# Three projection steps of an inverse's level together behind the masked product

## The chip, the cores and the metric

The kernel runs on one core of one Trainium2 chip. The metric is the device time of one execution in microseconds (us); three executions of the kernel before gave 1539.69 to 1544.26 us, median 1543.43. Engines: PE is TensorE (the matrix engine, with PEld its weight loads), DVE is VectorE, ACT is ScalarE, POOL is GpSimd, SP issues the DMAs.

## The reference, cut to what matters

The reference is one inference step of a decoder layer for a prompt of 512 tokens and 8 decode samples. The part that the change touches is the input projection and the RWKV-7 recurrence:

```
proj = h @ w_in                       # columns r | k | v | loras | pool | gates
xs   = cur + (prev_rows - cur) * mu_shift       # token shift
# per head, per token:
sa = S @ kk;  S = S*w - sa (kk*a)^T + v k^T;  y = S @ r
```

The prompt's recurrence is computed in chunks of 64 tokens. In a chunk the dependence of each token on the earlier ones is a unit triangular 64 x 64 matrix, which must be inverted, for 16 heads and 8 chunks.

## The kernel before, in words

The recurrence stage runs over c = 0..7, two heads (128 partitions) at a time; one turn of the loop is a **slot**, written out once for each engine in that engine's own order (functions `slot(c)` for PE, ACT, DVE and POOL). Engines wait for each other by counting semaphores only, and each engine takes its instructions in the order in which they are written. So what stands behind a waiting PE instruction waits too.

A slot on PE does two things at once. It computes the recurrence of head pair c in many small matrix products, whose results ACT, DVE and POOL have to take up before the next can run; and between these it projects the columns of the next pair, c + 1, which depend on nothing but the loaded weights. The projection is cut into **steps**: `kstep` is one of 8 slices of the contraction, six matmuls (fp32 split in a high and a low part), and there are three projections of 8 steps, 24 in all: steps 0 to 7 make K, 8 to 15 make R, 16 to 23 make V. `dense(n)` issues the next n steps. All three go to the same accumulation buffer, `PJ[0]`. So `project` waits at the first step of each (0, 8, 16) for two counts: `w_lo` (the weights are split) and `xs`, which DVE raises when it has finished reading the projection before out of `PJ[0]`. For step 8 that is the evacuation of K: two ACT operations (`shift`, lines 727 and 729) and one DVE operation (`XK`, line 870), in this order, and ACT starts once step 7 is done.

The **inverse** is built in levels lv = 0..5. Level lv from 1 on has:

- the masked product (`mm_x`, line 619), which needs `TI`, the transposed inverse, copied out by ACT at the level before (line 801), and the masked matrix `MO`, made by POOL;
- `dense(2)`; meanwhile DVE adds the identity to the product and writes `XI` (line 952; the trace names it RAW, whose memory it uses);
- at level 2 alone 16 small products (`mm_nv`);
- the wait for `XI`; the transpose's product (`mm_ti`, line 641, levels 1 to 4), from which ACT copies `TI`; and the inverse's product (`mm_tt`, line 645), from which DVE copies `TT` (line 962);
- an extra: at level 1 `center` (line 564) and at level 2 `variance` (line 568) of the pair before, from slot 1 on; at level 4 `ss` (line 520) of the next pair;
- `dense(1)`, at level 5 `dense(2)`.

After level 5 PE waits for `TT`, runs `mm_w` (line 659), one step (16, with the wait for R's evacuation), and after some products the chain of the eight states, with one step behind each of seven of them. At the slot's end ACT copies `WK` out (line 831), and PE's next slot waits for that. Slot 7 has no next pair: its `dense` does nothing. The projections ahead of slot 0 run one after the other with nothing between.

Of the kernel before, what the change touches and what calls it, by code (L numbers as in the profile page):

```python
# [46 lines left out]
LEVELS = 6  # L47
# [51 lines left out]
def build(nc, i, o):  # L99
    es = ExitStack()  # L100
    with es:
        sems = {}

        def S(name):
            if name not in sems:
                sems[name] = es.enter_context(nc.semaphore(name))
            return sems[name]
# [302 lines left out]
        with ExitStack() as sc:  # L410
# [47 lines left out]
            def num(c, q):  # L458
                return B_RKV + 3 * c + q
# [57 lines left out]
            def _(pe):  # L517
# [5 lines left out]
                def project(n, pj, k0, k1):  # L523
                    if k0 == 0:
                        pe.wait_ge(S("w_lo"), n + 1)
                        after(pe, "xs", n if n > 1 else 0)
                    for k in range(k0, k1):
                        mm = kstep(pe, PJ[pj], n % 3, k, Hh, Hl, k, k == 0, k == KT - 1, nb)
                    if k1 == KT:
                        mm.then_inc(S("prj"), 1)  # L530
# [9 lines left out]
                def za(c):  # L540
                    pe.wait_ge(S("sigw"), c + 1)
                    small(PJ[1], WL[64:P, :], TWA[64:P, :]).then_inc(S("mm_za"), 1)

                def ss(c):
                    pe.wait_ge(S("kks"), c + 1)
                    pe.wait_ge(S("alpha"), c + 1)
                    after(pe, "lnv", c - 1)
                    small(PJ[1], bones, SM[:]).then_inc(S("mm_ss"), 1)
# [12 lines left out]
                def center(c, nxt):  # L561
                    pe.wait_ge(S("yf"), c + 1)
                    pe.wait_ge(S("alpha"), c + 3) if nxt else pe.wait_ge(S("gte"), KT)
                    pe.matmul(PJ[1][:, 0, :], ctr, YF[:], start=True, stop=True).then_inc(S("mm_gn"), 1)

                def variance(c):
                    pe.wait_ge(S("yq"), c + 1)
                    pe.matmul(PJ[1][:, 1, :], bones, YQ, start=True, stop=True).then_inc(S("mm_gn"), 1)

                def slot(c):  # L570
# [3 lines left out]
                    def dense(n):  # L574
                        if not nxt:
                            return
                        for st in range(done[0], done[0] + n):
                            project(num(c + 1, st // KT), 0, st % KT, st % KT + 1)
                        done[0] += n
# [27 lines left out]
                    for lv in range(LEVELS):  # L607
                        if lv == 0:
                            pe.wait_ge(S("mo0"), c + 1)
                            pe.wait_ge(S("tr_ev"), 4 * c + 1)  # L610
                        else:
                            pe.wait_ge(S("mo"), (LEVELS - 1) * c + lv)
                            if lv == 1:
                                pe.wait_ge(S("xi"), LEVELS * c + 1)
                            else:
                                pe.wait_ge(S("ti"), (LEVELS - 2) * c + lv - 1)
                        for j in range(NJ):
                            for h in range(2):
                                mm = pe.matmul(B[0][HH[h], j * C:(j + 1) * C], MO[HH[h], lv % 2, j, :],  # L619
                                               I2[HH[h], :] if lv == 0 else TI[HH[h], j, :], start=True, stop=True)  # L620
                        mm.then_inc(S("mm_x"), 1)
                        if lv == 0:
                            if nxt:
                                za(c + 1)
                            continue
                        dense(2)
                        if lv == 2:
                            pe.wait_ge(S("tr_ev"), 4 * c + 4)
                            for j in range(NJ):
                                for h in range(2):  # L630
                                    mm = pe.matmul(B[3][HH[h], j * C:(j + 1) * C], KP[HH[1 - h], j, 0, :], VT[HH[1 - h], j, :],
                                                   start=True, stop=True)
                            mm.then_inc(S("mm_nv"), 1)
                        pe.wait_ge(S("xi"), LEVELS * c + lv + 1)
                        if lv == 1:
                            pe.wait_ge(S("tr_ev"), 4 * c + 3)
                        pe.wait_ge(S("tt"), LEVELS * c + lv)
                        if lv < LEVELS - 1:
                            for j in range(NJ):
                                for h in range(2):  # L640
                                    mm = pe.matmul(B[1][HH[h], j * C:(j + 1) * C], TT[HH[h], j, :], XI[HH[h], j, :], start=True, stop=True)
                            mm.then_inc(S("mm_ti"), 1)
                        for j in range(NJ):
                            for h in range(2):
                                mm = pe.matmul(B[2][HH[h], j * C:(j + 1) * C], XI[HH[h], j, :], TT[HH[h], j, :], start=True, stop=True)  # L645
                        mm.then_inc(S("mm_tt"), 1)
                        if lv == 1 and prv:
                            center(c - 1, nxt)
                        if lv == 2 and prv:
                            variance(c - 1)  # L650
                        if lv == 4 and nxt:
                            ss(c + 1)
                        dense(2 if lv == LEVELS - 1 else 1)

                    pe.wait_ge(S("tt"), LEVELS * (c + 1))
                    pe.wait_ge(S("nv_ev"), c + 1)
# [60 lines left out]
                for c in range(KT):  # L717
                    slot(c)
# [1083 lines left out]
```

## Time and profile before

| | |
|---|---|
| median of 3 executions | 1543.43 us |
| the profiled execution's own time | 1543.15 us |
| its span (first to last instruction) | 1541.4 us |
| PE busy | 1268.9 us, 82% of the span |
| DVE busy | 715.8 us, 46% |
| ACT busy | 471.1 us, 31% |
| POOL busy | 86.8 us, 6% |
| mean granted clock of TensorE | 0.920 |

The recurrence stage's eight slots last from about 198 to 676 us. Busy shares are means over stages with different limits; what one edit is worth is read in its own stage, from the order of starts on PE.

### The profile page before, as it was taken

How to read it: one execution, taken by the hardware profiler on the slowest of the kernel's cores; microseconds unless marked ns; L12 is line 12 of the kernel's file. 1: busy time of each engine (PE TensorE's matmuls, PEld its weight loads, DVE VectorE, ACT ScalarE, POOL GpSimd, SP SyncE). 2: the span in 40 equal slices, each digit the busy share in tenths (PEclk: the TensorE clock that was granted, in tenths of full speed). 3: DMA queues.
4: the chain of work that ended last, by engine and by line, in shares of the span. 5: the costliest groups of instructions: out<-in, count | busy, mean ns of one | idle time of the engine just before them, and what ended most of it. 6: DMA issues, size and time to landing. Idle time of an engine off the chain costs nothing. (4 is left out here: it accounts for less than half of the span.)

```text
span 1541.4 us, 33797 instructions
## 1 busy us (share of the span) xinstructions
PE 1268.9 (82%) x14732; PEld 1120.8 (73%) x14732; DVE 715.8 (46%) x1106; ACT 471.1 (31%) x715; POOL 86.8 (6%) x145
## 2 busy tenths in 40 slices
PE   4896799999999999857079999913999999789953
PEld 1225788888888888747079999913999989789952
DVE  2102455555555555435943333176566666632216
ACT  0003543333433334233032222303444444422211
POOL 0000021020220211201000000000000000000000
PEclk9996999999999999978589999955999999989985
DMA  8762011011010110012143232221232223133221
GB/s 271 261 230 73 14 47 48 2 48 47 3 47 4 46 34 3 3 51 76 55 125 93 84 93 79 82 115 49 76 91 81 88 82 94 38 89 100 75 83 61
DMA packets 160379, 117.17 MB, mean 76 GB/s; under 512 B 6240, under 2 KB 144278, under 8 KB 159975
## 3 DMA queue, kind: packets, MB, share of 16 engines
q1 hardware_dynamic: 160273, 115.57, 24.4%
q8 instruction: 89, 1.46, 0.4%
q14 instruction: 17, 0.14, 0.0%
HBM read 108.40 MB, written 7.34 MB: 75 GB/s over the span
## 5 line engine op out<-in xcount | busy, mean ns | idle before, releaser
L194 PE MATMUL PJ<-Hh,Wh 128*128 128x260 f32 (+1 forms) x1088 | 244.1, 306 | 53.3 <-DVE Wl L1683 18.9
L194 PEld LDWEIGHTS PJ<-Hh,Wh 128*128 128x128 f32 x1088 | 173.1, 194 | 72.8 <-issue 31.2
L194 PE MATMUL PJ<-Hl,Wh 128*128 128x260 f32 (+1 forms) x1088 | 224.2, 288 | 0.0
L194 PE MATMUL PJ<-Hh,Wl 128*128 128x260 f32 (+1 forms) x1088 | 223.1, 287 | 0.0
L194 PEld LDWEIGHTS PJ<-Hl,Wh 128*128 128x128 f32 x1088 | 173.0, 193 | 0.0
L194 PEld LDWEIGHTS PJ<-Hh,Wl 128*128 128x128 f32 x1088 | 172.7, 193 | 0.0
L1683 DVE TENSOR_TENSOR Wl<-RAW,Wh 128x1024 fp32r<-128x1024 f32 (+1 forms) x68 | 80.9, 1194 | 100.9 <-ACT Wh L1623 96.2
L1623 ACT ACTIVATE Wh<-RAW 128x1024 fp32r<-128x1024 f32 (+1 forms) x68 | 70.1, 1036 | 111.4 <-PE PJ L194 103.7
L1703 DVE SCALAR_TENSOR_TENSOR ACC<-ACC,CP 128x512 f32<-128x512 f32 x88 | 66.1, 751 | 69.6 <-ACT ACC L1634 68.0
L1377 DVE TENSOR_TENSOR Wl<-RAW,Wh 128x1024 fp32r<-128x1024 f32 (+1 forms) x40 | 44.7, 1119 | 112.8 <-ACT Wh L1339 112.0
L194 PE MATMUL PJ<-SFh,Wh 128*128 128x260 f32 x352 | 71.9, 286 | 14.5 <-DVE Wl L1683 14.5
L194 PE MATMUL BB<-Hh,Wh 128*128 128x260 f32 x352 | 71.6, 284 | 0.0
L194 PE MATMUL PJ<-SFl,Wh 128*128 128x260 f32 x352 | 71.4, 285 | 0.0
L194 PE MATMUL PJ<-SFh,Wl 128*128 128x260 f32 x352 | 71.4, 285 | 0.0
L194 PE MATMUL BB<-Hl,Wh 128*128 128x260 f32 x352 | 70.9, 283 | 0.0
L194 PE MATMUL BB<-Hh,Wl 128*128 128x260 f32 x352 | 70.7, 283 | 0.0
L194 PEld LDWEIGHTS PJ<-SFh,Wh 128*128 128x128 f32 x352 | 55.0, 191 | 14.7 <-issue 14.7
L1476 PE MATMUL PJ<-CST,ACC 128*128 128x128 f32 (+1 forms) x80 | 15.5, 364 | 60.4 <-DVE XA L1548 57.6
L1057 POOL TENSOR_TENSOR MO<-BP,CST 128x512 f32<-128x512 f32 x40 | 54.5, 1362 | 104.1 <-PE BB L619 101.9
L962 DVE COPY TT<-BB 128x512 f32<-128x512 f32 x40 | 27.6, 691 | 66.2 <-PE BB L645 66.2
L1476 PEld LDWEIGHTS PJ<-CST,ACC 128*128 128x128 f32 (+1 forms) x80 | 11.5, 170 | 63.9 <-DVE XA L1548 59.7
L194 PEld LDWEIGHTS PJ<-SFl,Wh 128*128 128x128 f32 x352 | 55.1, 190 | 0.0
(305 smaller groups left out, 2421.0 us busy)
## 6 DMA issues: line engine op xcount, KB each, us to landing
RAW<-in_w_in_dram SPq DMA_DIRECT2D x46, 512.0 KB, 4.1
RAW<-in_ffn_up_dram SPq DMA_DIRECT2D x44, 512.0 KB, 3.8
RAW<-in_ada_w_dram SPq DMA_DIRECT2D x6, 2048.0 KB, 8.4
ACC<-in_ada_w_dram SPq DMA_DIRECT2D x6, 2048.0 KB, 8.0
RAW<-in_ffn_down_dram SPq DMA_DIRECT2D x16, 512.0 KB, 4.1
RAW<-in_w_branch_rwkv_dram SPq DMA_DIRECT2D x8, 512.0 KB, 4.1
RAW<-in_w_out_dram SPq DMA_DIRECT2D x8, 512.0 KB, 4.0
RAW<-in_ffn_down_dram SPq DMA_DIRECT2D x8, 384.0 KB, 3.4
```

Of the source, the lines that this page charges most:

```text
L194: mm = pe.matmul(out[:, b, 0:nb[b]], w[:, slot, kw, :], x[:, kx, c0:c0 + nb[b]], start=first and w is Wh and x is xh, stop=last and w is Wl)
L962: dve.tensor_copy(TT[:], bank8(2)).then_inc(S("tt"), 1)
L1057: pool.tensor_tensor(MO[:, lv % 2], BP[:, :, 0, :], rows8(CST[:, C_OFF + C * lv:C_OFF + C * (lv + 1)]), ALU.mult).then_inc(S("mo"), 1)
L1377: dve.tensor_tensor(Wl[:, slot, 0:kn], RAW[:, slot, 0:kn], Wh[:, slot, 0:kn].bitcast(F32), ALU.subtract).then_inc(S("w_lo"), 1)
L1476: mm = pe.transpose(PJ[t % 2][0:n, b, r * P:(r + 1) * P], delta[:, k, t * P:t * P + n], ident)
L1623: act.activation(Wh[:, slot, 0:kn], RAW[:, slot, 0:kn], ACT.Copy).then_inc(S("w_hi"), 1)
L1683: dve.tensor_tensor(Wl[:, slot, 0:kn], RAW[:, slot, 0:kn], Wh[:, slot, 0:kn].bitcast(F32), ALU.subtract).then_inc(S("w_lo"), 1)
L1703: dve.scalar_tensor_tensor(cv[:, 0:T], u[:, k:k + T], w, cv[:, 0:T], ALU.mult, ALU.add)
```

## The change

Two numbers. In levels 1 to 5 the first `dense` issues three steps instead of two, and the one behind the inverse's product issues none instead of one (levels 1 to 4), or one instead of two (level 5). The 24 steps of a slot, their order and the rest of the slot stay. The count by the end of each level is as before: 3, 6, 9, 12, 16.

```diff
                         if lv == 0:
                             ...
                             continue
-                        dense(2)
+                        dense(3)
                         if lv == 2:
                             ...
                         if lv == 4 and nxt:
                             ss(c + 1)
-                        dense(2 if lv == LEVELS - 1 else 1)
+                        dense(1 if lv == LEVELS - 1 else 0)
```

## Rows read from the trace of the kernel before

**Rows 1.** Windows, one slot: us, busy (count) per engine, PEclk, DMA share, GB/s.

```profile
320.00:382.00 62.00, 59.80 (x1132) 52.84 (x1135) 33.66 (x51) 22.43 (x36) 9.17 (x13) 1.00 0.11 31
```

**Rows 2.** Waits of PE from 200 to 630: us in total, times, longest.

```profile
PE BB L590 <- ACT WK L831: 9.1, 6, 1.5
...
PE BB L619 <- ACT TI L801: 1.9, 7, 0.3
```

**Rows 3.** Timeline of PE, slot 2, level 3: start, us, engine, line, operation.

```profile
342.39 1.15 PE L619 MATMUL BB<-TI,MO 64*64 64x64 f32 x32
343.47 0.51 PE L194 MATMUL PJ<-Hh,Wh 128*128 128x260 f32 x2
...
345.12 1.15 PE L641 MATMUL BB<-RAW,TT 64*64 64x64 f32 x32
...
347.16 0.48 PE L194 MATMUL PJ<-Hh,Wh 128*128 128x260 f32 x2
...
348.41 1.15 PE L619 MATMUL BB<-TI,MO 64*64 64x64 f32 x32 [0.27 <-ACT TI L801]
```

**Rows 4.** Timeline of ACT and DVE there: the evacuation of K.

```profile
345.23 0.70 ACT L727 ACTIVATE A<-PJ,PV 128x520 f32<-128x520 f32 x1 [4.35 <-PE PJ L194]
...
346.26 0.76 DVE L870 SCALAR_TENSOR_TENSOR XK<-PJ,OM,A 128x520 f32<-128x520 f32 x1 [1.98 <-ACT A L729]
```

**Rows 5.** Timeline ahead of slot 0: an evacuation between two projections.

```profile
161.41 0.76 DVE L870 SCALAR_TENSOR_TENSOR AL<-PJ,OM,A 128x520 f32<-128x520 f32 x1 [3.22 <-ACT A L729]
162.32 0.48 PE L194 MATMUL PJ<-Hh,Wh 128*128 128x260 f32 x2 [1.98 <-DVE AL L870]
```

**Rows 6.** Timeline of slot 0, levels 1 and 2, which have no extra.

```profile
210.22 1.10 PE L645 MATMUL BB<-TT,RAW 64*64 64x64 f32 x32
211.25 0.51 PE L194 MATMUL PJ<-Hh,Wh 128*128 128x260 f32 x2
...
212.17 1.15 PE L619 MATMUL BB<-TI,MO 64*64 64x64 f32 x32
```

**Rows 7.** Timeline of slot 7, level 3, where `dense` does nothing.

```profile
650.62 1.15 PE L641 MATMUL BB<-RAW,TT 64*64 64x64 f32 x32 [0.79 <-DVE RAW L952]
...
651.82 0.60 ACT L801 ACTIVATE TI<-BB 128x512 f32<-128x512 f32 x1 [3.92 <-PE BB L641]
...
652.56 1.15 PE L619 MATMUL BB<-TI,MO 64*64 64x64 f32 x32
```

**Rows 8.** Timeline, `center` in slot 7 without steps, then in slot 2 with one.

```profile
642.62 1.13 PE L564 MATMUL PJ<-YF,CTR 128*128 128x512 f32 x2
643.67 0.97 PE L619 MATMUL BB<-TI,MO 64*64 64x64 f32 x26
...
333.32 1.13 PE L564 MATMUL PJ<-YF,CTR 128*128 128x512 f32 x2
...
335.10 1.15 PE L619 MATMUL BB<-TI,MO 64*64 64x64 f32 x32
```

**Rows 9.** Timeline of slot 2, level 4: `ss`, and level 5's masked product.

```profile
353.17 1.14 PE L520 MATMUL PJ<-SM,CST 128*128 128x260 f32 x4
...
354.98 1.15 PE L619 MATMUL BB<-TI,MO 64*64 64x64 f32 x32
```

**Rows 10.** Timeline, level 5's end in slot 2, then in slot 7 without steps.

```profile
357.71 1.15 PE L645 MATMUL BB<-TT,RAW 64*64 64x64 f32 x32
...
360.45 1.96 PE L659 MATMUL BB<-AW,TT 64*64 64x128 f32 x32
...
658.36 1.15 PE L645 MATMUL BB<-TT,RAW 64*64 64x64 f32 x32 [0.78 <-DVE RAW L952]
...
660.30 0.87 PE L659 MATMUL BB<-AW,TT 64*64 64x128 f32 x12 [0.79 <-DVE TT L962]
```

**Rows 11.** Timeline of ACT at slot 2's end: the evacuation of V.

```profile
380.05 0.70 ACT L727 ACTIVATE A<-PJ,PV 128x520 f32<-128x520 f32 x1 [4.61 <-PE PJ L194]
```

**Rows 12.** Windows, the start of slot 5; columns as in rows 1.

```profile
506.00:509.00 3.00, 3.00 (x61) 2.67 (x53) 1.74 (x4) 0.00 (x0) 1.14 (x6) 0.52 0.73 202
```

## The prediction

> **What bounds the kernel now.** I read the windows by slot first, then who PE waits for, then the order of starts on PE in one slot, and last the evacuations on ACT and DVE beside it. In slot 2 PE is busy 59.8 us of 62 [rows 1], and in this stretch PE waits longest for the slot's end; inside the levels it waits only for `TI`, 0.27 us a slot [rows 2]. The reader is to see two things there. PE sets the pace, so time added to or taken from PE's own order is added to or taken from the kernel. And no wait for `XI` stands in the list of PE's waits for slots 0 to 6: two steps already cover it. A third step in that place has no wait to remove.
>
> The stall-free picture has one tight place, level 3. Step 7, the last of K, ends there at 345.12, and step 8, the first of R, starts at 347.16 [rows 3]. Between the two PE runs the transpose's and the inverse's product. In the same time ACT (345.23) and then DVE (346.26, 0.76 long) read K out of `PJ[0]`, until 347.02 [rows 4]. Step 8 may not start before this read is over. In the kernel before, the two products hide the evacuation, with 0.14 us to spare.
>
> **The change, part by part.** No instruction is added or removed; five steps a slot are moved, on PE alone, in slots 0 to 6. No DMA and no SP or POOL instruction is moved.
>
> Durations of the blocks. One step between small products costs 0.92 us (211.25 to 212.17 [rows 6]); two cost 1.65 (343.47 to 345.12 [rows 3]); so a further step in an existing block costs about 0.73.
>
> *Level 3.* Step 8 now stands right behind step 7 and must wait for the evacuation. The row that shows such a wait by itself is the one ahead of slot 0, where a projection follows another with nothing between: PE sat idle 1.98 us, and went on at 162.32, 0.15 after DVE's end at 162.17 [rows 5]. In slot 2, counted from the start of level 3's masked product (342.39), K is out at 4.63, so step 8 starts at 4.78 and ends 0.90 later at 5.68. I take 0.90 and not 0.92 since a step after a wait has a first group of 0.48 and not 0.51 [rows 3, 5]. Then come the transpose's and the inverse's product, and the next masked product directly. Slot 7 shows this sequence without any step: 650.62 to 652.56, 1.94 [rows 7]. The masked product of level 4 so starts at 5.68 + 1.94 = 7.62, where it started at 6.02 before (348.41 - 342.39 [rows 3]). That is 1.60 us later. The 0.27 that it waited for `TI` before is gone inside these numbers: in slot 7 the copy of `TI` starts 1.20 after the transpose's product and takes 0.60, which just fits into the 1.94 [rows 7].
>
> Bounds of this term: if the weights of the waiting step were loaded already, 0.15 less; if `TI` came as late as before, 0.27 more. 1.45 to 1.87, and I take 1.60.
>
> *Levels 1, 2 and 4, slots 1 to 6.* Here the moved step stood behind an extra. `center` with a step behind it took 333.32 to 335.10, 1.78 [rows 8]; `center` without one 1.05 in slot 7 [rows 8]. The difference, 0.73, is just what the step costs in its new place. No gain, no loss. `variance` at level 2 repeats the pattern. For `ss` with its step the trace has 1.81 (353.17 to 354.98 [rows 9]) and none without a step; 1.81 less one step of 0.92 to 0.73 gives 0.89 to 1.08 for it alone. The level changes by -0.19 to 0, and I take 0, by the nearest row, `center`.
>
> *Levels 1 and 2, slot 0.* Without an extra, the inverse's product plus a step took 212.17 - 210.22 = 1.95 [rows 6]. Without the step it takes 0.93: the 1.94 of rows 7 for both products, less 1.01 for the transpose's (2.04 for both in rows 3, less 1.03 for the inverse's in rows 6). That saves 1.02 and the third step costs 0.73: -0.29 each, -0.58 together.
>
> *Level 5.* Behind the inverse's product one step is left of two. `mm_w` needs `TT`, and slot 7 shows how late that is: 1.94 after the inverse's product, 0.79 of it idle [rows 10]. Product and one step take 2.74 - 0.73 = 2.01 [rows 10], so the copy is still covered, by 0.07. Were it not, 0.1 a slot. The three steps in front cost the 0.73 that is taken away behind. Step 15, which ends R, stays the instruction in front of `mm_w`, so R's evacuation and step 16's wait for it keep their distance.
>
> *What else might come late.* Level 4's `XI`: DVE has `TT` of level 3, two products for the key and `XI` in a row, four operations no longer than the 0.76 of rows 4. From the end of the inverse's product, at about 7.75 in the count above, they end by 10.8; PE asks for `XI` after the masked product and three steps, at 7.62 + 1.08 + 2.38 = 11.1. Covered. ACT's roots end earlier than R's evacuation starts by about a microsecond. After level 5 every wait is counted from PE's own work: ACT sat idle 4.61 us for PE before it read V out [rows 11], so the wait for `WK` moves along unchanged.
>
> **The sum.** Slots 1 to 6: 6 x 1.60 = 9.60. Slot 0: 1.60 - 0.58 = 1.02. Together 10.6 us, all on PE's order, against the profiled execution's own 1543.15: 1553.8. The median of the runs shown lies 0.3 above this execution, so I say 1554. Later stages start from the last slot and shift as a whole.
>
> **A rule against it: the clock.** The granted clock was 1.00 throughout slot 2 [rows 1], and it stayed at full speed after the 1.98 idle of rows 5: the next steps ran at their usual pace. But after the idle at slot 5's start it fell to 0.52 for some 3 us [rows 12]. By the Trainium skill, page "TensorE: Matmul & The Clock Gate", section "Why this matters for your kernels", idle gaps between bursts of matmuls send the array back to half rate. The trace bears this out at one of the slots' ends, with 1.5 us idle before it; the windows of the six other slots from 0 to 6 repeat the 1.00 of rows 1. The new gap of 1.9 is a second such place in each slot.
>
> **The rivals.**
>
> *Clock (0.08).* The clock falls at each of the seven new gaps. Price: half of 3 us at 0.52, 1.4 each [rows 12], 10 in all, on top of 10.6: 1564. For it: rows 12. Against it: rows 5, the very same gap with steps on both sides, and the six slots at 1.00.
>
> *The extras hide the seam (0.05).* The rise is smaller because behind `center`, `variance` and `ss` the seam of a block falls away as it does in slot 0: 18 places (three levels, six slots) of 0.29, less 5.2 us: 1549. For it: rows 6. Against it: rows 8 measure the place itself.
>
> *The slot's end absorbs it (0.05), the other side.* PE waits 1.5 for `WK` at each slot's end [rows 2]. If ACT's end of the slot were set by ACT's or DVE's own queue and not by PE, PE could be 1.5 late for nothing: 10.6 less 7 x 1.5 gives 1543, no change. It decides at one point: whether the copy of `WK` stays put when PE is late. Against it: the 4.61 idle of ACT for PE [rows 11].
>
> *The wait is not there (0.02), faster.* If the count that step 8 asks for were met already, level 3 would be one block of three: 1.08 + 2.38 + 1.94 = 5.40 against 6.02, -0.62 in seven slots, and -0.58 in slot 0: -4.9, 1538.3. Against it: rows 5, where DVE's read is what PE was released by.
>
> **How the numbers follow.** The forecast, 1554, has 0.80. Its own range is 1.45 to 1.87 a slot (9.6 to 12.6 us), the seam of `ss` (up to -1.3), level 5 (up to +0.7), and one clock fall more or less in an execution (1.4 each way; the runs of before span 4.6): 1550 to 1559. It leaves the clock rival out above and the others below, some 0.2 together. What a measurement can tell from no change is 0.3%, 4.6 us. Slower holds the forecast, the clock and the seams: 0.92. Same holds the absorption and half of what is odd: 0.05. Faster: 0.03.
>
> **What would show it.** In each of slots 0 to 6 a new wait of PE for DVE's `XK` at level 3, seven in number, 1.8 to 1.9 us each, 13 in sum. The wait for `TI` (1.9 in 7) gone. From level 3's masked product to level 4's 7.6 and not 6.0. Slots of 63.5 and not 61.9. Slot ends with the same 1.5 for `WK`. The forecast is wrong if `XK`'s evacuation ends earlier relative to step 7, if the wait for `WK` shrinks, if a seam behind an extra gives time back, or if the windows at level 3 show a clock under 1.

## The result

The changed kernel takes 1559.5 us in the median of four executions (1554.76, 1558.15, 1560.92, 1564.52) against 1543.8 before: a ratio of 1.011, interval 1.007 to 1.015. In a second comparison the changed kernel's median over five more executions is 1559.54 again, against 1542.26 for 17 of the kernel before; a third one, without the changed kernel, has 22 of the kernel before at 1541.68. So the change costs 15.7 us in the first comparison and 17.3 in the second, where 10.6 were forecast. The direction, the place and the wait are as forecast; the size is not, and the range (to 1559) missed it by half a microsecond.

The profiled execution of the changed kernel (its own time 1554.76, span 1553.0) agrees with the forecast to a microsecond, 11.6 over that of before. That is luck, as the times by stage below show: one must look into the stage that was changed, and not at the two spans.

Who PE waits for in the changed kernel, from 195 to 650, answers to [rows 2]:

```profile
PE PJ L194 <- DVE XK L870: 13.8, 7, 2.0
PE BB L590 <- ACT WK L831: 10.6, 7, 1.5
PE BB L666 <- DVE W L973: 2.3, 7, 0.3
```

The first line is new, in each of the seven slots with a next pair, 1.97 us each (forecast 1.8 to 1.9). `WK`'s wait is the same 1.52 a slot (the 9.1 of [rows 2] were for six, this is for seven). The wait for `TI` is gone.

PE in slot 2, level 3, answers to [rows 3]:

```profile
345.49 1.15 PE L619 MATMUL BB<-TI,MO 64*64 64x64 f32 x32
346.57 0.52 PE L194 MATMUL PJ<-Hh,Wh 128*128 128x260 f32 x2
...
350.27 0.48 PE L194 MATMUL PJ<-Hh,Wh 128*128 128x260 f32 x2 [1.97 <-DVE XK L870]
...
351.17 1.15 PE L641 MATMUL BB<-RAW,TT 64*64 64x64 f32 x32
352.15 1.10 PE L645 MATMUL BB<-TT,RAW 64*64 64x64 f32 x32
...
353.11 1.15 PE L619 MATMUL BB<-TI,MO 64*64 64x64 f32 x32
```

Step 8 starts 4.78 after the level's masked product, the two products follow it at 5.68, and level 4's masked product starts at 7.62: to the hundredth the working of the prediction. DVE's part of the evacuation, answering to [rows 4], ends at 350.13, 0.14 before step 8:

```profile
349.37 0.76 DVE L870 SCALAR_TENSOR_TENSOR XK<-PJ,OM,A 128x520 f32<-128x520 f32 x1 [1.99 <-ACT A L729]
```

`center` with no step behind it takes 337.12 to 338.18, 1.06 (forecast 1.05 [rows 8]). Level 5's copy of `TT` stays hidden, as worked out from [rows 10]: 2.00 from the inverse's product to `mm_w`, with no wait.

```profile
337.12 1.12 PE L564 MATMUL PJ<-YF,CTR 128*128 128x512 f32 x2
338.18 1.15 PE L619 MATMUL BB<-TI,MO 64*64 64x64 f32 x32
...
363.11 1.15 PE L645 MATMUL BB<-TT,RAW 64*64 64x64 f32 x32
365.11 1.96 PE L659 MATMUL BB<-AW,TT 64*64 64x128 f32 x32
```

Now the same place in slot 0:

```profile
218.53 0.48 PE L194 MATMUL PJ<-Hh,Wh 128*128 128x260 f32 x2 [1.97 <-DVE XK L870]
218.84 0.41 PE L194 MATMUL PJ<-Hl,Wh 128*128 128x260 f32 x2
219.09 0.58 PE L194 MATMUL PJ<-Hh,Wl 128*128 128x260 f32 x2
219.60 1.98 PE L641 MATMUL BB<-RAW,TT 64*64 64x64 f32 x32
221.37 1.64 PE L645 MATMUL BB<-TT,RAW 64*64 64x64 f32 x32
222.85 1.10 PE L619 MATMUL BB<-TI,MO 64*64 64x64 f32 x32
```

The wait is as long, but half a microsecond after step 8 has begun, the operations get longer: the transpose's product takes 1.77 and not 0.98 to the next. The windows (us, busy and count by engine, granted clock, DMA) show why, slot 0 first, then slot 2:

```profile
218.00:221.00 3.00, 2.47 (x32) 2.27 (x34) 0.38 (x1) 0.73 (x1) 0.00 (x0) 0.69 0.00 0
...
351.00:354.00 3.00, 3.00 (x96) 2.86 (x97) 0.70 (x2) 1.54 (x2) 0.00 (x0) 1.00 0.02 5
```

The granted clock averages 0.69 in slot 0's window: for a part of it TensorE ran at the lower of its two levels, 1.2 GHz and not 2.4. In slot 2 it did not. Such a change to the lower level is called a fall here. Counting the falls by the starts of the masked products (level 3's to level 4's is 7.6 without and 9.1 with one; a slot's last to the next slot's first is 33.4 without and 35.0 with one, 32.4 and 33.8 for slot 6) gives the whole account. "Slots" is from slot 0's first masked product to slot 7's, in the profiled execution; each profile is of one execution, the median of all:

| kernel | falls at level 3 | falls at slot ends | slots, us | median, us |
|---|---|---|---|---|
| before | 0 | 1 (slot 4) | 432.5 | 1541.7 |
| before, second profile | 0 | 1 (slot 6) | 432.0 | |
| changed | 3 (0, 5, 6) | 3 (0, 1, 2) | 450.6 | 1559.5 |
| changed, second profile | 3 (0, 5, 6) | 3 (0, 1, 2) | 450.6 | 1559.5 |
| step 8 put back | 0 | 2 (0, 3) | 433.6 | 1540.3 |
| level 3 alone | 2 (0, 3) | 3 (0, 3, 4) | 450.8 | 1559.2 |
| gap filled | 0 | 3 (4, 5, 6) | 446.0 | 1556.9 |
| gap longer | 7 | 4 (0, 2, 4, 6) | 462.8 | 1571.5 |
| before, ends filled | 0 | 0 | 430.8 | 1538.3 |
| changed, both filled | 0 | 0 | 441.6 | 1549.4 |
| new order on ACT | 0 | 0 | 423.9 | 1532.9 |

The medians come from three comparisons, in which the kernel before had 1543.8, 1542.3 (changed again, step 8 put back, level 3 alone, gap filled) and 1541.7 (the last four of the table), so a difference across them is good to a microsecond or two, and the slots' times are the sharper measure.

The stage itself lost 450.6 - 432.5 = 18.1 us: 10.6 by the new wait, as forecast, and 7.5 by five more falls of 1.5. In the first pair of profiles 4.1 of it were hidden by a slow start of the kernel before (its slot 0 began at 204.20, in its second profile at 200.39; the changed kernel's at 200.07 and 202.09) and 2.4 by stages after the slots, which the change does not touch.

### The profile page after: what moved, and what is told of

Read it like the earlier page. It is cut to its first block and busy times, and to the rows that moved or that the text cites. A ratio compares the mean times of both kernels' runs of the same rounds, so it can differ in the third digit from the quotient of the medians.

```text
span 1553.0 us, 33797 instructions
## 1 busy us (share of the span) xinstructions
PE 1271.1 (82%) x14732; PEld 1122.2 (72%) x14732; DVE 715.8 (46%) x1106; ACT 472.0 (30%) x715; POOL 85.6 (6%) x145
## 3 DMA queue, kind: packets, MB, share of 16 engines
q8 instruction: 89, 1.46, 0.4%
## 5 line engine op out<-in xcount | busy, mean ns | idle before, releaser
L194 PE MATMUL PJ<-Hh,Wh 128*128 128x260 f32 (+1 forms) x1088 | 237.7, 300 | 66.7 <-DVE Wl L1683 18.8
```

The costliest lines, as they stand in the source:

```text
L194: mm = pe.matmul(out[:, b, 0:nb[b]], w[:, slot, kw, :], x[:, kx, c0:c0 + nb[b]], start=first and w is Wh and x is xh, stop=last and w is Wl)
```

## The experiments

**Put step 8 back.** Levels 1, 2, 4 and 5 changed, level 3 as before.

```diff
-                        dense(3)
+                        dense(2 if lv == 3 else 3)
...
-                        dense(1 if lv == LEVELS - 1 else 0)
+                        dense(1 if lv in (3, LEVELS - 1) else 0)
```

> The changed kernel with one step put back: at level 3 two steps in front and one behind the inverse's product, as before; levels 1, 2, 4 and 5 stay changed. Theory 1 (all of the loss is the wait of step 8 for K's evacuation, and the clock falls that this gap brings): the time of the kernel before less 0.6 us, 1543, with the spread of the kernel before (about 5 us), and no wait of PE for XK. Theory 2 (part of the loss lies in the three joined steps of the other levels): 2 to 6 us above the kernel before, 1546 to 1550.

Measured 1540.3 against 1542.3 (ratio 0.998, 0.997 to 0.999), twelve executions from 1536.1 to 1541.8. In PE's waits `XK` does not appear, and `TI` is back:

```profile
PE BB L590 <- ACT WK L831: 10.6, 7, 1.5
PE BB L666 <- DVE W L973: 2.4, 7, 0.3
PE BB L619 <- ACT TI L801: 1.9, 7, 0.3
```

So all of the loss is at level 3. The joined steps of the other levels cost nothing. The two levels of slot 0 did give their share: 5.49 and 6.16 us, against 5.67 and 6.42 in the second profile of the kernel before. The gain of 2.0 us is more than the 0.6 worked out, and the interval (1.1 to 4.9 us) does not reach down to 0.6. Falls do not explain the rest, since this profile has two and those of the kernel before have one each; what does is open.

**Level 3 alone.**

```diff
-                        dense(2)
+                        dense(3 if lv == 3 else 2)
...
-                        dense(2 if lv == LEVELS - 1 else 1)
+                        dense(2 if lv == LEVELS - 1 else 0 if lv == 3 else 1)
```

> The kernel before with level 3 alone changed (three steps in front, none behind). Theory 1: 7 x 1.60 = 11.2 us from the wait, plus clock falls at the new gap of 1.5 us each in some of the seven places, so 1555 to 1565, spread about 10 us, as the changed kernel. Theory 2: 2 to 6 us less than the changed kernel.

Measured 1559.2 (1555.75 to 1563.8), ratio 1.011, 1.009 to 1.014: the changed kernel's loss. One step moved in one level of seven slots costs what the whole change costs. Its profile has one fall fewer and yet the same 450.8 us in the slots: level 4 takes 6.70 us and not 6.55, since with two steps in front the inverse's product waits a little for `XI`, and slot 0's levels 1 and 2 do not give their 0.6.

**The changed kernel again.**

> The changed kernel once more, to see how its executions spread and to have a second profile. Theory 1: median 1556 to 1562; from level 3's masked product to level 4's either 7.6 or 9.1 us in each slot, the 9.1 in other slots than in the first profile (0, 5 and 6 there), with a granted clock under 1 there. Rival (falls belong to certain slots, say to their DMAs): the 9.1 again in slots 0, 5 and 6.

Measured 1559.54 (1558.38 to 1560.62). The half of the expectation on where the falls are was wrong: they are in the very same places as in the first profile, 0, 5 and 6 at level 3 and the ends of 0, 1 and 2. They are not spread at random. But neither are they bound to these slots: with level 3 alone changed they come in 0 and 3. This profile also has the place of [rows 5], the gap of 1.97 ahead of slot 0, and here the clock does fall behind it (0.50 in the window):

```profile
158.41 0.49 PE L194 MATMUL PJ<-Hh,Wh 128*128 128x260 f32 x2 [1.97 <-DVE AL L870]
```

```profile
160.00:163.00 3.00, 3.00 (x16) 3.00 (x15) 2.46 (x3) 1.46 (x2) 0.00 (x0) 0.50 0.00 0
```

So it does, 1.4 to 1.5 us behind that gap, in five of the eleven profiles. The row on which the forecast took the falls as zero does not show the rule, but one of two outcomes that both occur.

**Fill the gap.** Ahead of step 8 (`KT` is 8) PE does useless work in the time that it would wait: 14 matmuls into the other accumulation buffer, which nobody reads. The three waits in front are for that buffer and the weights.

```diff
                         for st in range(done[0], done[0] + n):
+                            if st == KT:
+                                pe.wait_ge(S("w_lo"), num(c + 1, R_) + 1)
+                                pe.wait_ge(S("alpha"), c + 2)
+                                after(pe, "lnv", c)
+                                for _ in range(14):
+                                    pe.matmul(PJ[1][:, 1, 0:260], Wh[:, num(c + 1, R_) % 3, 0, :], Hh[:, 0, 0:260], start=True, stop=True)
```

> The changed kernel, with 14 matmuls of 128x260 whose result nobody reads in the new gap, between step 7 and the wait of step 8. They take 14 x 0.122 = 1.7 us, less than the 1.97 of the gap, so step 8 starts when it did. Theory 1: the 10.6 us of the wait stay, the clock falls at the gap go: median 1554 to 1556, spread near the kernel before's, and level 3's masked product to level 4's is 7.6 in all seven slots. Rival (the excess over 10.6 us is not the clock, or falls are not brought by the idle gap): median 1559 and a spread of 10 us, as the changed kernel.

Slot 0 in this kernel, the filler at 219.00:

```profile
216.37 1.15 PE L625 MATMUL BB<-TI,MO 64*64 64x64 f32 x32
...
219.00 1.83 PE L583 MATMUL PJ<-Hh,Wh 128*128 128x260 f32 x14
221.14 0.48 PE L194 MATMUL PJ<-Hh,Wh 128*128 128x260 f32 x2 [0.31 <-DVE XK L876]
...
222.05 1.15 PE L647 MATMUL BB<-RAW,TT 64*64 64x64 f32 x32
...
223.98 1.15 PE L625 MATMUL BB<-TI,MO 64*64 64x64 f32 x32
```

Step 8 starts 4.77 after the masked product, as without the filler, and the next masked product at 7.61, in all seven slots. The falls at level 3 are gone, and the slots are 4.6 us shorter than in the changed kernel, three falls' worth. Three falls remain at the slots' ends, which this kernel does not fill, as many as the changed kernel has there. The median, 1556.9 (1550.9 to 1558.1), fell by 2.7 alone and lies a microsecond above the expected 1554 to 1556; with five and six executions this is not resolved further.

**A longer gap.**

```diff
                         for st in range(done[0], done[0] + n):
+                            if st == KT:
+                                pe.wait_ge(S("kks"), c + 2)
```

> The changed kernel with a longer gap: step 8 also waits for ACT's square of the key, which ends 0.76 us after the read of K (347.78 against 347.02 in the kernel before's slot 2). Theory 1 (each gap costs its length, and brings a clock fall of 1.5 us the more often the longer it is): 7 x 0.76 = 5.3 us over the changed kernel's 1559.5 by the wait alone, and more than the three of seven gaps with a fall, up to seven: 1565 to 1571; level 3's masked product to level 4's is 8.4 without and 9.9 with a fall. Rival (a fall goes with certain places in time, not with the length of the gap): 5.3 us and no more falls, 1564 to 1565.

Measured 1571.5 (1565.4 to 1575.2), 12.0 over the changed kernel and half a microsecond above the expected range. In the slots it is 12.2: the waits grew from 13.8 to 18.5, 4.7 and not the 5.3 expected, and there are five more falls of 1.5. PE's waits first, then windows in slot 1 before, in and after the gap:

```profile
PE PJ L194 <- ACT SM L760: 18.5, 7, 2.6
```

```profile
281.00:284.00 3.00, 2.85 (x45) 2.53 (x44) 1.38 (x2) 0.11 (x1) 1.29 (x1) 1.00 0.00 0
284.00:287.00 3.00, 0.50 (x4) 0.51 (x5) 0.76 (x1) 1.58 (x3) 0.00 (x0) 1.00 0.00 0
287.00:290.00 3.00, 3.00 (x57) 2.85 (x57) 0.00 (x0) 0.74 (x2) 0.00 (x0) 0.62 0.02 5
```

The clock is 1.00 in the gap and falls after it. All seven gaps of 2.64 us bring a fall, where 1.97 brought three of seven. The rival, that length does not matter, is out; that the place in time matters too is shown further on.

**Fill the slots' ends, in the kernel before and, with the filler of level 3, in the changed one.**

```diff
                     mm.then_inc(S("t_wk"), 1)
+                    if nxt:
+                        pe.wait_ge(S("gte"), c + 2)
+                        for _ in range(10):
+                            pe.matmul(PJ[1][:, 1, 0:260], Wh[:, num(c + 1, R_) % 3, 0, :], Hh[:, 0, 0:260], start=True, stop=True)
```

> The kernel before with 10 matmuls of 128x260, read by nobody, behind each slot's last product, in the 1.52 us in which PE waits for WK. They take 1.2 us. The kernel before's profile has one clock fall there in seven. Theory 1: none here, every slot 61.9, time 1 to 2 us under the kernel before's, 1540 to 1541.5. Rival (filling changes nothing): 1542.3.

> The changed kernel with both gaps filled, the one of level 3 and the one at the slot's end. Theory 1: no clock fall among the slots 0 to 6, each of 1 to 5 takes 63.5 us, and the time over that of the kernel before with its slot ends filled is the bare wait, 7 x 1.60 less 0.6, 10.6 us, so 1551 to 1553. Rival (something else than wait and clock falls): the difference stays at 14 us or more.

The kernel before with its ends filled: 1538.3 (ratio 0.998, 0.996 to 1.000). The changed kernel with both filled: 1549.4, and its waits of PE are

```profile
PE BB L672 <- DVE W L983: 2.4, 7, 0.3
PE PJ L194 <- DVE XK L880: 2.2, 7, 0.3
...
PE BB L596 <- ACT WK L841: 0.4, 2, 0.2
```

Neither has a fall between slot 0 and slot 7. Their difference is 11.1 in the medians and 441.6 - 430.8 = 10.8 in the slots: the bare wait, forecast as 10.6. What the changed kernel loses to falls is then 450.6 - 441.6 = 9.0 in the slots, six falls of 1.5 (10.1 in the medians), and the kernel before 1.7 and 1.2 in its two profiles (3.4 in the medians). Both filled kernels came out 1.6 to 1.7 below their expected ranges (1540 to 1541.5 and 1551 to 1553), while the slots took what was expected.

**The kernel before, a second profile.**

> The kernel before once more, for a second profile of its clock falls at the slots' ends (one of seven in the first). With its ends filled it was 3.4 us faster in the median, which at 1.6 us a fall is two of them: so one to three falls of seven here, none inside the levels (level 3's masked product to level 4's 6.02 in all), and 432 to 436 us from slot 0's first masked product to slot 7's. If there is none, the 3.4 us of the filling came from somewhere else.

One fall, at slot 6's end, 432.0 in the slots. So falls explain 1.2 to 1.7 of the 3.4 that the filling gave; the rest is inside that ratio's interval (0.5 to 5.9 us) and its cause is open.

**A version that beats both.** Step 8 as before the change, and on ACT:

```diff
-                        shift(num(c + 1, V_), 0, mu(c + 1, V_))
                     act.wait_ge(S("mm_y"), c + 1)
                     ...
                     act.activation(WK[:], B[2][:, 0:C], ACT.Copy).then_inc(S("wk"), 1)
+                    if nxt:
+                        shift(num(c + 1, V_), 0, mu(c + 1, V_))
```

> A version that should beat both: step 8 behind the inverse's product as in the run with one step put back (1540.3), and on ACT at the slot's end YF and WK copied ahead of the evacuation of V, not behind it. PE's next slot then starts 1.0 us earlier (380.75 instead of 381.79 in slot 2), as long as the evacuation of V, 0.5 us later, does not hold up DVE's first masks of the next slot, which have about 1 us of slack. Theory: 7 x 1.0 = 7 us less, and fewer clock falls at the shorter gap: 1531 to 1534. If the masks are late instead: 1537 to 1541.

Measured 1532.9 (1531.6 to 1537.7), ratio 0.995, 0.994 to 0.997. ACT at slot 1's end, answering to [rows 11]: `WK` is now copied ahead of V's evacuation, not behind it.

```profile
310.76 0.60 ACT L827 ACTIVATE YF<-BB 128x512 f32<-128x512 f32 x1 [3.69 <-PE BB L696]
311.94 0.22 ACT L830 ACTIVATE WK<-BB 128x64 f32<-128x64 f32 x1 [0.58 <-PE BB L704]
312.06 0.69 ACT L727 ACTIVATE A<-PJ,PV 128x520 f32<-128x520 f32 x1
```

PE's wait is

```profile
PE BB L590 <- ACT WK L830: 2.9, 7, 0.4
```

2.9 us in seven in place of 10.6, a slot takes 60.88 and not the 61.93 of the kernel with step 8 put back, and there is no fall at a gap this short, 0.42 us.

## Why the prediction was wrong

*What bounds the kernel* held: PE sets the pace, and all that is added to its order appears in the time.

*Level 3* held to the hundredth (4.78, 5.68, 7.62), with its release row from [rows 5] and its sequence without steps from [rows 7]. Only the "0.14 us to spare" is misread: PE goes on 0.14 after DVE's end in the changed kernel too, where it waits, and 0.15 after in [rows 5]. So this is the time from the release to the first matmul, and the kernel before had nothing to spare: its two products fit the evacuation exactly. *Levels 1, 2 and 4* held: 1.06 for `center`, 6.54 for level 4 to 5 against 6.57. *Slot 0* gave 0.27 and 0.24 for the 0.29 each (second profile of before, 5.67 and 6.42, against 5.40 and 6.18). *Level 5* held. *The wait for `WK`* moved along unchanged, so the absorption rival is out, and so are the hidden seams and the missing wait. The clock rival came true by near half: three falls at the seven new gaps, each at about the price it named. The sum, 10.6, is what the two filled kernels differ by, 10.8 to 11.1.

What failed is the step "a rule against it: the clock". The sum has no term for the falls, the range allows one more or less, and five more came, 7.5 us in the slots. The last of its own signs of being wrong, a clock under 1 in the windows at level 3, is what showed. The sum took them as zero because one gap of 1.98 in the trace of before, ahead of slot 0 [rows 5], had brought none, and the rival that priced them knew only seven falls or none, at 0.08. The trace held the other half of the evidence: a gap of 1.5, shorter than the new one, had brought a fall [rows 12]. So a gap of that kind must be priced by a share of a fall, not by yes or no. The runs give the shares in the slots: no fall in seven gaps of 0.4 us; in those of 1.5, one in seven in each profile of the kernel before and two to four in the variants, 20 of 56 in all; three, three and two in seven at 1.97; seven in seven at 2.64. With three falls at 1.5 added the forecast would have been 1558. The other two come from the unchanged gaps at the slots' ends, where the changed kernel has three falls and the kernel before one.

Why these rise can be read from the traces, though no run was made to test it. In each profile the falls begin at times that lie on one even grid. Where a gap ends against this grid decides, with no exception among the 77 gaps of 1.5 and 1.97: a gap of 1.52 brings a fall when the next time of the grid comes between 0.06 before its end and 0.55 after it (the nearest without a fall have 0.12 before and 0.62 after), a gap of 1.97 when it comes 0.26 to 1.05 after (the nearest without, 0.24 before and 1.74 after). For the 2.64 it is 0.26 to 1.46. So a longer gap is hit more often, and how often a row of gaps is hit depends on the length of the slots between them. At the ends of the changed kernel's slots 0, 1 and 2 the falls begin at 256.70, 321.55 and 386.40, 64.85 apart, and a slot with such a fall takes 65.1: so the fall comes 0.50 after the first gap, 0.22 after the second and 0.06 before the end of the third, and misses the fourth. In the kernel before a slot without a fall takes 61.90, which shifts the gap by 0.46 against the grid from slot to slot, and one with a fall 63.54, which moves it out of reach at once: one fall. Two profiles whose slots lie alike against the grid, as the changed kernel's two do (delays of 0.50, 0.22 and -0.06 in one, 0.55, 0.26 and 0.01 in the other), have the same falls.

The rule that was cited (the Trainium skill, "TensorE: Matmul & The Clock Gate", section "Why this matters for your kernels": idle gaps between bursts send the array back to half rate) agrees with the longer gap's seven of seven, and the filler shows that it is the idleness and not the wait that does it. The section has longer gaps in mind than any of these; here gaps of 1.5 us brought falls too, and the measurement decides.

## What to carry to other kernels

Where PE sets the pace, a block of work that separates two uses of one accumulation buffer is not filler that can be moved freely: it hides the evacuation, here 2.04 us of products over 1.90 of ACT and DVE and the 0.14 until PE goes on. Before joining blocks, ask which of them is the first to need a buffer again, and leave that one where it is. And price an idle gap of TensorE at its length plus a share of a clock fall, the larger the longer it is, with a wide range: gaps that recur at even distances are hit in runs or not at all. A gap that cannot be closed can be shortened by putting the copy that PE waits for first in its engine's order.

## What the runs showed of the hardware that was not expected

The falls can repeat: two profiles of the changed kernel, whose slot 0 began at 200.07 and 202.09, have all six in the same places; those of the kernel before do not (slot 4, then slot 6). A fall costs 1.4 to 1.6 us of this work, and begins at the gap's end or later: from 0.06 us before it to 0.55 after for the gaps of 1.5, up to 1.46 after for those of 2.64. In the longer gap's kernel the window that holds the gap has a clock of 1.00 and the next 0.62. Useless matmuls in a gap are free as long as they end before the wait does: step 8 starts at 4.77 with the filler and at 4.78 without. In both gaps they were worth 9.0 us of the changed kernel's slots.
